# The prompt's mLSTM in rounds between pairs of heads of the prompt's attention, in a one-layer decoder kernel

## The reference

```python
def step(carry, xs):                     # one chunk of tokens
    b = cumsum(log forget gate)
    dmat = where(causal, b[:, None] - b[None, :] + ig[None, :], -inf)
    m_t = maximum(b + m_st, max(dmat, -1))
    w_intra = exp(dmat - m_t)
    a = w_intra * (q @ k.T)
    num = a @ v + (q @ c_st) * w_inter
    den = max(abs(sum(a) + w_inter * (n_st . q)), exp(-m_t))
    h = num / den
    c_new = sc * c_st + (wk * v).T @ k   # n_new alike
...
mix_m = sigmoid(m_o) * head_norm(h)
```

## Time and profile before

| | |
|---|---|
| time, median of three runs | 999.06 us (998.09 to 1001.32) |
| the profiled execution: time, span | 997.98 us, 996.0 us |
| mean granted clock of TensorE | 0.91 of full speed |
| PE, PEld busy | 890.6 us (89%), 803.7 us (81%) |
| DVE, ACT, POOL busy | 594.0 us (60%), 405.7 us (41%), 135.6 us (14%) |
| prompt's attention | from 310.55 to 423.95 us of the span |
| prompt's mLSTM up to the reciprocal of the deviation | from 423.95 to 481.39 us |

### The profile page before, as it was taken

The page is one execution under the profiler, slowest core; times in us unless marked ns, Lnnn a source line. Parts: engine busy times, 40 slices in busy tenths (PEclk is TensorE's granted clock), DMA queues, the critical chain, the costliest instruction groups (busy, mean ns, idle before and its releaser), DMA issues.

```text
span 996.0 us, 20070 instructions
## 1 busy us (share of the span) xinstructions
PE 890.6 (89%) x7843; PEld 803.7 (81%) x7843; DVE 594.0 (60%) x1227; ACT 405.7 (41%) x769; POOL 135.6 (14%) x248
## 2 busy tenths in 40 slices
PE   5989989898898888887587999999999999899994
PEld 5988877777786555566457999999999999899993
DVE  4522246431414677556755857888888888656465
ACT  4322345534513456510103426555555555212223
POOL 2012223243350000030020001111111111000000
PEclk9989999889997698975557999999999999999997
DMA  8248687677555000000205322222222222133222
GB/s 303 65 139 269 221 278 213 204 232 210 165 153 200 1 2 1 2 1 6 91 1 214 135 67 85 86 86 86 86 90 94 91 87 75 56 93 94 77 70 90
DMA packets 54704, 112.46 MB, mean 113 GB/s; under 512 B 6969, under 2 KB 32346, under 8 KB 54162
## 3 DMA queue, kind: packets, MB, share of 16 engines
q1 hardware_dynamic: 46168, 89.06, 27.4%
q0 software_dynamic: 6528, 17.83, 5.9%
q10 hardware_dynamic: 1914, 4.29, 1.2%
HBM read 105.54 MB, written 12.40 MB: 118 GB/s over the span
## 4 chain that ended last, share of the span: by engine, by line
PE 78%; DVE 10%; issue 3%; DMA 3%; ACT 3%; POOL 1%; SPq 0%; ACTq 0%; POOLq 0%; DVEq 0%
PE q L1852 30%; PE q L1850 27%; DMA arena<-in_pool 3%; PE q L2170 2%; PE q L2188 2%; PE q L1914 2%; PE q L2198 2%; PE q L2277 1%; PE q L1902 1%; PE q L2328 1%; DVE xt L1414 1%; PE q L1968 1%; ACT whi L977 1%; PE q L1925 1%; PE q L2240 1%
## 5 line engine op out<-in xcount | busy, mean ns | idle before, releaser
L1850 PE MATMUL q<-arena_r,whi_r 128*128 128x256 f32 x712 | 212.6, 299 | 24.0 <-DVE xt_r L496 11.6
L496 DVE TENSOR_TENSOR wring_r<-wring,whi_r 128x1024 fp32r<-128x1024 f32 (+1 forms) x101 | 120.1, 1190 | 189.3 <-ACT whi_r L493 189.0
L1852 PE MATMUL q<-arena_r,whi_r 128*128 128x288 f32 (+1 forms) x712 | 214.5, 301 | 0.0
L1852 PE MATMUL q<-arena_r,wring_r 128*128 128x288 f32 (+1 forms) x712 | 214.0, 301 | 0.0
L1850 PE MATMUL q<-arena_r,wring_r 128*128 128x256 f32 x712 | 203.0, 285 | 0.0
L493 ACT ACTIVATE whi_r<-wring 128x1024 fp32r<-128x1024 f32 (+1 forms) x101 | 104.4, 1033 | 232.4 <-PE q L1852 209.3
L1852 PE MATMUL q<-xt_r,whi_r 128*128 128x290 f32 (+1 forms) x552 | 166.2, 301 | 0.0
L1850 PEld LDWEIGHTS q<-arena_r,whi_r 128*128 128x128 f32 x712 | 138.0, 194 | 31.4 <-issue 20.2
L1850 PE MATMUL q<-xt_r,whi_r 128*128 128x256 f32 x552 | 157.1, 285 | 0.0
L1852 PEld LDWEIGHTS q<-arena_r,whi_r 128*128 128x128 f32 x712 | 138.1, 194 | 0.1
L1850 PEld LDWEIGHTS q<-arena_r,wring_r 128*128 128x128 f32 x712 | 137.7, 193 | 0.0
(11 more groups left out here) (446 smaller groups left out, 1600.6 us busy)
## 6 DMA issues: line engine op xcount, KB each, us to landing
wring<-in_w_up SPq DMA_DIRECT2D x42, 512.0 KB, 3.3
wring<-in_w_in SPq DMA_DIRECT2D x27, 512.0 KB, 5.1
arena<-in_pool SPq DMA_DIRECT2D x64, 192.0 KB, 3.6
arena<-in_pool POOLq DMA_DIRECT2D x64, 192.0 KB, 4.1
wring<-in_w_down SPq DMA_DIRECT2D x24, 448.0 KB, 3.3
arena<-in_pool POOLq DMA_DIRECT2D x64, 64.0 KB, 2.6
arena<-in_pool SPq DMA_DIRECT2D x64, 64.0 KB, 2.4
wring<-in_w_out SPq DMA_DIRECT2D x8, 512.0 KB, 9.5
```

Of the source, the lines that this page charges most:

```text
L496: return eng.tensor_tensor(out, src, hi.bitcast(F32), ALU.subtract)
L1850: pe.matmul(out[:, 0, 0:HALF], w, x[:, 0:HALF], start=(kk == 0 and n == 0), stop=(end and n == 2))
L1852: mm = pe.matmul(out[:, 1, 0:width - HALF], w, x[:, HALF:width], start=(kk == 0 and n == 0), stop=(end and n == 2))
```

## The change

The loop of the prompt's mLSTM after the attention is gone. Its steps are now issued inside the attention's loop, one chunk for each query tile. In the step of pair 0, 2, 4 and 6 of a tile PE does the exponents, the states (the chunk's new state, and the product with the carried one), the scores and the values of the chunk. ACT takes the exponential in the step of pair 1, out of PSUM. DVE does `carry`, `products` and `divided` in the steps of pairs 3, 5 and 7, and the centring and the variance in pairs 0 and 2 of the next tile. All of a chunk's products use banks 2 and 3, one after another. So the attention's scores have banks 0 and 1 alone: the scores of a pair wait for the logits of the pair before (`np_x`), where they waited for those of the pair before that. DVE's minimum with the causal table is replaced on PE: the product of an identity matrix with the table is added to the exponents in PSUM. The buffers move to free space (`smem`, two regions of `zt`), and POOL's weighting of the values runs ahead of the attention. The copies to `rescale` do too.

```diff
         ctv = smem[:, 0:2048].rearrange("p (c n) -> p c n", c=4)
         vexp = smem[0:32, 2048:4096].rearrange("p (s c) -> p s c", s=4)
...
-        comb = work[:, 0:520].rearrange("p (q t e) -> p q t e", q=2, t=4)
-        sq = work[:, 520:1032].rearrange("p (h d) -> p h d", h=H)
-        carried = work[:, 1040:1560].rearrange("p (s t e) -> p s t e", s=2, t=4)
+        wx = smem[:, 2048:3072]
+        comb = smem[:, 3072:3592].rearrange("p (q t e) -> p q t e", q=2, t=4)
+        sq = smem[:, 3592:4104].rearrange("p (h d) -> p h d", h=H)
+        carried = zt[:, Z_G, 0:520].rearrange("p (s t e) -> p s t e", s=2, t=4)
...
-        wv = arena[:, 4640:6720].rearrange("p (i h c) -> p i h c", i=4, h=H)
+        wv = zt[:, Z_SV:Z_CV + 1, :].rearrange("p k c -> p (k c)")[:, 0:2080].rearrange("p (i h c) -> p i h c", i=4, h=H)
...
-            pool.wait_ge(np_pv, PAIRS)
+            pool.wait_ge(tok_k_ev, 2 * (QT + 1))
+            pool.wait_ge(stored, 16 * 3)
...
                 if i >= 2:
                     masked_rows(i)
 
-            pool.wait_ge(ml_v, QT)
+            pool.wait_ge(np_pv, PAIRS)
             pool.memset(qm, 0.0).then_inc(sd_qz, 1)
...
-
-            for c in range(QT):
-                act.wait_ge(ml_x, c + 1)
-                act.activation(whi_f[:, c % 2, :], whi_f[:, c % 2, :], ACT.Exp).then_inc(ml_w, 1)
+                if m < PAIRS and c == 1:
+                    act.wait_ge(ml_d, i + 1)
+                    act.activation(wx, q4[1].rearrange("p b c -> p (b c)"), ACT.Exp).then_inc(ml_w, 1)
...
-                    ins = dve.tensor_tensor_reduce(out=pb[:, slot, g, 0:w], in0=bank[2 * (m % 2) + g][:, 0:w],
+                    ins = dve.tensor_tensor_reduce(out=pb[:, slot, g, 0:w], in0=bank[g][:, 0:w],
...
+            rescale = s4[:, 16:32]
+
+            def by_token_row(c0, n, t):
+                return q4[1][:, :, c0:c0 + n].rearrange("p q (t e) -> p q t e", t=t)
+
+            def carry(c):
+
+                dve.wait_ge(ml_st, c + 1)
+                new = by_token_row(260, 130, 2)
+                kept, made = (carried[:, s % 2].rearrange("p (b t) e -> p b t e", b=2) for s in (c, c + 1))
+                if c == 0:
+                    dve.tensor_copy(made, new).then_inc(ml_ce, 1)
+                    return
+                link(dve.tensor_tensor(comb, by_token_row(0, 260, 4), bc(by_head(emp[:, 96 + 8 * c:104 + 8 * c]), HD + 1),
+                                       ALU.mult))
+                link(dve.tensor_tensor(made, kept, bc(rescale[:, 4 * c:4 * c + 4].rearrange("p (b t) -> p b t", b=2), HD + 1),
+                                       ALU.mult))
+                dve.tensor_tensor(made, made, new, ALU.add).then_inc(ml_ce, 1)
+
+            def products(c):
+                dve.wait_ge(ml_s, c + 1)
+                dve.wait_ge(ml_w, c + 1)
+                dve.scalar_tensor_tensor(out=wx, in0=q4[1].rearrange("p b c -> p (b c)"), scalar=QS, in1=wx,
+                                         op0=ALU.mult, op1=ALU.mult).then_inc(ml_a, 1)
+
+            def divided(c):
+
+                dve.wait_ge(ml_v, c + 1)
+                num = by_token_row(0, 260, 4)
+                if c >= 1:
+                    dve.tensor_tensor(comb, comb, num, ALU.add).then_inc(ml_cb, 1)
+                    dve.wait_ge(ml_cb, c + 1)
+                    num = comb
+                d, r = (s4[:, n:n + 8].rearrange("p (q t) -> p q t", q=2) for n in (0, 8))
+                link(dve.tensor_scalar(d, num[:, :, :, HD], -1.0, None, ALU.mult))
+                link(dve.tensor_tensor(d, d, num[:, :, :, HD], ALU.max))
+                link(dve.tensor_tensor(d, d, by_head(emp[:, 8 * c:8 * c + 8]), ALU.max))
+                link(dve.reciprocal(r, d))
+                hv = hc[:, c, :, :].rearrange("p (t q) d -> p q t d", q=2)
+                ins = dve.tensor_tensor(hv, num[:, :, :, 0:HD], bc(r, HD), ALU.mult)
+                if c == 0:
+                    ins.then_inc(ml_cb, 1)
+                    dve.wait_ge(ml_cb, 1)
+                else:
+                    link(ins)
+
+            def centred_heads(c):
+                hv, s8 = hc[:, c, :, :], s4[:, 0:8]
+                link(dve.tensor_reduce(s8, hv, AX, ALU.add))
+                link(dve.scalar_tensor_tensor(out=hv, in0=bc(s8, HD), scalar=-1.0 / HD, in1=hv,
+                                              op0=ALU.mult, op1=ALU.add))
+
+            def head_variance(c):
+                link(dve.tensor_tensor(sq, hc[:, c, :, :], hc[:, c, :, :], ALU.mult))
+                dve.tensor_reduce(var[:, 8 * c:8 * c + 8], sq, AX, ALU.add).then_inc(ml_n, 1)
+
+            mlstm = (None, carry, products, divided)
+            dve.wait_ge(g_em, 1)
+            for q in range(2):
+                p = slice(64 * q, 64 * q + 64)
+                ins = dve.tensor_copy(rescale[p].rearrange("p (c t) -> p c t", t=4),
+                                      emp[p, 128:160].rearrange("p (c t q) -> p q c t", t=4, q=2)[:, q])
+            link(ins)
             for g in range(GROUPS):
                 dve.tensor_copy(mixt[:, 4:8, T + 16 * g:T + 16 * g + 16], mixd[:, g])
             cmp_scores(0)
                         cmp_scores(i + 1)
                     if c == 4:
                         cmp_probs(i + 1)
+                if m % 2 == 1 and c > 1:
+                    mlstm[c // 2](i)
+                elif c == 0 and i >= 1:
+                    centred_heads(i - 1)
+                elif c == 2 and i >= 1:
+                    head_variance(i - 1)
+            head_variance(QT - 1)
             mixed(QT - 1)
...
-            def decay(c):
-                dve.wait_ge(ml_d, c + 1)
-                dve.tensor_tensor(by_block(whi_f[:, c % 2, :]), by_block(q4[0].rearrange("p b c -> p (b c)")),
-                                  causal.unsqueeze(1).broadcast_to([128, H, 128]), ALU.min).then_inc(ml_x, 1)
...
-            decay(0)
-            carry(0)
-            products(0)
-            for c in range(QT):
-                if c + 1 < QT:
-                    decay(c + 1)
-                normed(c)
-                if c + 1 < QT:
-                    carry(c + 1)
-                    products(c + 1)
...
-                if m >= 2:
-                    pe.wait_ge(np_x, m - 1)
+                if m >= 1:
+                    pe.wait_ge(np_x, m)
                 w = 128 * i + 128
                 for g in range(NG):
-                    mm = pe.matmul(bank[2 * (m % 2) + g][:, 0:w], q_of(GQ * g + j, i),
+                    mm = pe.matmul(bank[g][:, 0:w], q_of(GQ * g + j, i),
...
+            def token_rows(c):
+                return slice(128 * c, 128 * c + 128)
+
+            def exponents(c):
+
+                pe.wait_ge(ml_r, c + 1)
+                if c >= 1:
+                    pe.wait_ge(ml_cb, c)
+                for q in range(2):
+                    pe.matmul(bank[2 + q], gl[:, token_rows(c)], rows[:, c % 2, 512 * q:512 * q + 512],
+                              start=True, stop=False)
+                    mm = pe.matmul(bank[2 + q], ident, causal.unsqueeze(1).broadcast_to([128, 4, 128]),
+                                   start=False, stop=True)
+                mm.then_inc(ml_d, 1)
+
+            def states(c):
+                pe.wait_ge(ml_w, c + 1)
+                pe.wait_ge(ml_wv, c + 1)
+                for t in range(4):
+                    for q in range(2):
+                        h, at = 2 * t + q, 260 + 65 * (t % 2)
+                        mm = pe.matmul(bank[2 + t // 2][64 * q:64 * q + 64, at:at + 65], tk[:, c, HD * h:HD * h + HD],
+                                       wv[:, c, h, :], start=True, stop=True)
+                if c >= 1:
+                    pe.wait_ge(ml_ce, c)
+                    for t in range(4):
+                        for q in range(2):
+                            p = slice(64 * q, 64 * q + 64)
+                            mm = pe.matmul(bank[2 + q][:, 65 * t:65 * t + 65], zt[p, Z_MQ + t, token_rows(c)],
+                                           carried[p, c % 2, t, :], start=True, stop=True)
+                mm.then_inc(ml_st, 1)
+
+            def scores(c):
+                pe.wait_ge(ml_ce, c + 1)
+                for t in range(4):
+                    for q in range(2):
+                        p = slice(64 * q, 64 * q + 64)
+                        mm = pe.matmul(bank[2 + q][:, 128 * t:128 * t + 128], zt[p, Z_MK + t, token_rows(c)],
+                                       zt[p, Z_MQ + t, token_rows(c)], start=True, stop=True)
+                mm.then_inc(ml_s, 1)
+
+            def values(c):
+                pe.wait_ge(ml_a, c + 1)
+                for t in range(4):
+                    for q in range(2):
+                        mm = pe.matmul(bank[2 + q][:, 65 * t:65 * t + 65], wx[:, 512 * q + 128 * t:512 * q + 128 * t + 128],
+                                       tv[:, c, 2 * t + q, :], start=True, stop=True)
+                mm.then_inc(ml_v, 1)
+
+            mlstm = (exponents, states, scores, values)
...
```

(59 more changed lines are left out.)

57 lines of the change are left out of this document (removed).

## The result

| | before | after |
|---|---|---|
| time, median | 998.58 us (996.11 to 1001.32) | 972.44 us (965.35 to 975.09) |
| ratio, 95% interval | | 0.9726 (0.9669 to 0.9784) |
| the profiled execution: time, span | 997.98, 996.0 us | 971.89, 969.9 us |
| mean clock | 0.91 | 0.935 |

The busy time by stage of the kernel after shows where the time went: the four query tiles (the last in two parts, up to the start of its last scores and up to the reciprocal), then everything behind. Its columns are those of the earlier trace rows: from:to, the length, the busy time of PE, PEld, DVE, ACT and POOL with the number of instructions, the granted clock, and the DMA share and GB/s.

The account below looks back on a forecast made before the run. The prediction took a serial mLSTM stage that no engine fills, and an attention loop paced by a chain of waits, as the bound: -57.4 + 44 - 1 = -14.4, so 997.98 us becomes 983.6 us, range 973 to 994.

Parts of the forecast that it names:

- What goes: Serial mLSTM loop over four chunks, from the last attention eviction to the reciprocal: all 57.4 us leave.
- TensorE's rounds charged in full: PE's four rounds per query tile lie on the attention's chain: 8.65 us a tile at full clock, 16.1 at half.
- the upper bound: Exponents: identity product costs as much again as the 40-row product, 2.0 us at full clock or 3.4 at half.
- The terms of the chain in the prediction: Last tile: scores 1.1, logits 1.5, exponentials 1.4, copy 1.1, values 1.0, transposes 1.0, said to make 7.2 us.
- Which clock?: Rounds priced by each tile's earlier clock: first at half 12.6 us, second 12.4, third 10.2, last at full 8.65.
- The sum of 44: PE's rounds over all four query tiles add 43.85 us, taken as 44.
- full-clock price of 8.65: One query tile's exponents, states, scores and values on PE cost 8.65 us at full clock.
- "clock stays full" rival: All rounds run at full clock and fill pauses, costing 33.6 - 1.5 us: 971.7 us; chance 0.18.
- Behind the loop: Transposes of the normed rows may find a better clock: gain between 0 and 2.0 us, taken as 1.
- DVE hidden, banks free, ACT free: In the attention's loop, DVE's steps, one pair of score banks and ACT's exponential were all charged nothing.
- lost cover that I kept 5 us for: First three tiles: the carry delays the next logits; the stall absorbs most, 5 us kept for the upper bound.
- the 3.8 us that I worked out by it: GpSimd's two masked rows inside the loop could block DVE at their shared port, adding up to 3.8 us.

Follow-up runs that it names:

- run 1: Changed kernel without the identity products, so without the causal bound, ratio to the kernel before: 968.27 us, 0.9715.
- run 2: Changed kernel with each identity product made twice, ratio to the kernel before: 988.35 us, 0.9856.
- run 9: Changed kernel with DVE's minimum kept for the causal bound, so no identity product on PE, ratio to the kernel before: 971.12 us, 0.9719.
- run 11: Changed kernel as it is, repeated as a single traced execution: 984.25 us.
- run 3: Kernel before with the attention's scores on one pair of banks: 997.33 us, ratio 1.0013.
- run 4: Kernel before, mLSTM still in series, with the identity product in place of DVE's minimum: 1009.34 us, ratio 1.0129.
- run 6: Kernel before with ACT's copy of the transposes ahead of its exponentials: 984.46 us, ratio 0.9857.
- run 12: Changed kernel as it is, repeated once more as a single traced execution: 986.63 us.
- run 7: Changed kernel with DVE's square in the variance made three times instead of once, ratio to the kernel before: 980.04 us, 0.983.

## Why the prediction was right, and where it was wrong

**What goes: right.** The chain between the last eviction and the reciprocal is gone, as this timeline of DVE after shows: eviction at 453.59, reciprocal at 454.20.

```profile
453.59 0.69 DVE L1433 COPY mixt<-q 128x512 f32<-128x512 f32 x1 [2.26 <-PE q L2168]
454.20 0.34 DVE L1527 RECIPROCAL var<-var 128x32 f32<-128x32 f32 x1
454.58 2.29 DVE L1528 TENSOR_TENSOR zt<-zt,var 128x2048 f32<-128x2048 f32 x1
```

**TensorE's rounds charged in full: right.** The last tile, the only one whose clock was steady in all four executions of the changed kernel, grew by 8.85 us where 8.65 stood. By parts, each up to the next instruction: exponents 4.2 for 3.9, states 1.6 for 1.7, scores 1.0 for 1.2, values 1.8 for 1.85. The identity product does not overlap the 40-row one: each pair of records takes 1.05 us up to the next, so the upper bound was the right one to take. Runs 1, 2 and 9 confirm the charge at equal clock. At half clock the exponents were charged too little: eight records took 8.0 us in run 11's second tile (343.73 to 351.75), where 6.9 stood. (The terms of the chain in the prediction add up to 7.1 us, not 7.2; nothing hangs on it.)

**"Which clock?": this is the step that failed.** From the earlier trace rows I charged the first three tiles 12.6, 12.4 and 10.2 us. The profiled execution showed 9.6, 6.9 and 7.4: 11.3 us less, nearly all of the miss. The sum of 44 was not a wrong price for the work: the executions of 986.63 and 984.25 us show 43.4 and 46.4, and their time is the forecast's 983.6 to within some 3 us. In the execution of 986.63 us the tiles agree one by one as well: 12.4, 13.95, 8.2 and 8.8 us of growth for 12.6, 12.4, 10.2 and 8.65. In that of 984.25 us they do not; there the second tile's 17.7 makes up for the third tile's 7.4, so that its nearness to 44 is partly luck.

The error was to read each tile's clock of one trace of the kernel before as a property of the tile. It is an outcome: in the second tile of the changed kernel 0.95, 0.95, 0.68 and 0.59, hence growth from 6.9 to 17.7 us. In the kernel before and its variants (runs 3, 4, 6) the same tile had 0.65 to 0.77, a narrower spread that one trace did not show at all. When the clock rises at the end of the first tile, the tile's own work gains too, so that 6.9 is below even the full-clock price of 8.65; so does the third tile's 7.4, at 0.95 for 0.88. That 10.2 was too much in every one of the four executions, by 2.0 to 2.8 us.

Known only now, the ten times suggest a forecast with two cases, 972 and 985 us, and a range from 965 to 988. My "clock stays full" rival gave 971.7, 0.7 below the measured median, but that is luck: its premise did not come true, since the first tile stayed at 0.63. Against the charges 3.0 us were gained in the first tile, 5.5 in the second and 2.8 in the third.

The rule that back-to-back matmuls hold the full clock (Trainium skill, page "TensorE: Matmul & The Clock Gate", section "Loop structure matters more than you think") is not borne out. In run 11 PE was busy for 35.83 of 36.06 us on end, across the border of the first and second tile, and the clock stayed at half:

```profile
328.94:365.00 36.06, 35.83 (x173) 21.27 (x173) 18.22 (x78) 11.58 (x48) 1.89 (x1) 0.50 0.00 0
```

The second tile's shares, 39.97 of 42.03 us at clock 0.59 in run 11 and 26.65 of 31.24 at 0.95 in the profiled execution, say less: a slower clock itself makes the same work busier.

**Behind the loop: the gain is not there.** I took 1 us of gain in the sixteen transposes of the normed rows. They take 3.90 us as before, at half clock, after a wait of 3.47 us for DVE's multiply, and the same in runs 11 and 12:

```profile
457.01 3.90 PE L2286 MATMUL q<-cst,zt 128*128 128x128 f32 x16 [3.47 <-DVE zt L1528]
```

The stretch from the reciprocal on took 515.7 us for 514.6; in the runs above it lies between 514.5 and 517.0, so the 1.1 is drift.

**DVE hidden, banks free, ACT free: right for the kernel as it is**, by run 3 and by its own waits: the scores wait for DVE three times in the loop, 1.9 us in all (0.92 of it in the first tile, at 320.83), the transposes 0.4 and the exponents 0.2. That is what shows of the lost cover that I kept 5 us for. The cover is thin, though: DVE work added in runs 7 and 9 reached PE as waits of 1.99, 1.01 and 0.55 us and of 1.74.

**GpSimd beside DVE.** DVE's timeline after, while GpSimd's masked row ran from 318.86 to 320.75 and its multiply from 320.83 to 321.89:

```profile
320.10 0.68 DVE L1419 TENSOR_SCALAR xt<-xt 128x2 f32<-128x2 f32 x1
...
320.88 1.34 DVE L1428 TENSOR_SCALAR xt<-xt,gcol 128x128 f32<-128x128 f32 x2
...
322.95 0.60 DVE L1428 TENSOR_SCALAR xt<-xt,gcol 128x128 f32<-128x128 f32 x2
```

A negated maximum of 0.17 us took 0.68 and ended with the masked row; the two gating steps took 1.34 for 0.60. Beside the second masked row another took 0.41. The delays are 1.5 us. PE's waits for DVE right behind them are 0.92 and 0.39 us in the first tile and 0.69 in the second; how much of these is GpSimd's doing is not shown, as no run leaves its work out. The Trainium skill's rule (page "SBUF — State Buffer", section "Who interferes with whom") agrees in kind; the 3.8 us that I worked out by it were too many, because for most of both masked rows DVE was idle or ran logits, which took no longer (0.29 us each in the first tile).

## What to carry to other kernels

A serial stage whose engines wait for each other is worth moving between the steps of another loop even if that loop's busiest engine takes it in full: here 57.4 us left, 33 to 46 came. Price such a move at TensorE's full and half clock, and where the tiles stand between the two, look at several traces, or give both as cases, before choosing one number. Then ask whether a step should go to the engine on the path at all: DVE's minimum was free in the second and the last tile and cost a wait of 1.7 us in the first, while TensorE's identity product cost 1.9 to 3.9 us in every tile, and much less in bf16. The order of ACT's two steps was worth 11 us of the loop (146.1 to 134.8), against the 26 us of the whole change. And a step that is hidden may have little room left: look for the wait that appears when it is made longer.

## What the runs showed of the hardware

- The granted clock of one stretch differs between executions of the same program: second tile 0.59 to 0.95, 31.24 to 42.03 us, the program's time 965 to 987 us (on one chip 0.59 and 0.68).
- A high busy share of PE did not bring the full clock: busy for 35.83 of 36.06 us, at 0.50 throughout (run 11). What does decide stays open; no run here varied it by itself.
- A float32 product of 512 columns takes 1.05 us at full clock, with 40 rows of weights or with 128; the bf16 one 0.32, and it adds into a bank between float32 products.
